# Two decoder layers in one kernel: the up projection's low part of x joins a 512-column product, relative biases are loaded by pairs of heads, and an mLSTM signal is sent earlier

## The reference

```python
# feed-forward of layer one, D_FF = 2816
h = rmsnorm(x, g_ffn) @ w_up                     # (256, 5632)
h = causal_depthwise_conv(h, conv_w, width=3) + conv_b
gate, up = split(h, 2)
y = (gelu(gate) * up) @ w_down

# block attention, S = one block of 256
logits = q @ k.T / 8 + table[:, rel_bucket(q_pos - k_pos)]   # causal
p = softmax(logits)

# mLSTM, per head, after num/den and a norm per head
y_h = (norm(h) * head_norm_g + skip * conv) * silu(z)
```

## Time and profile before

| | us |
|---|---|
| median of 3 runs | 782.49 (782.23 to 783.82) |
| profiled execution, its own time | 784.3 |
| its span, first to last instruction | 782.5 |
| PE busy | 771.3 (99%) |
| DVE busy | 568.2 (73%) |
| ACT busy | 439.1 (56%) |
| POOL busy | 151.0 (19%) |

### The profile page before, as it was taken

The page is one execution under the profiler, slowest core; times in us unless marked ns, Lnnn a source line. Parts: engine busy times, 40 slices in busy tenths (PEclk is TensorE's granted clock), DMA queues, the critical chain, the costliest instruction groups (busy, mean ns, idle before and its releaser), DMA issues.

```text
span 782.5 us, 12013 instructions
## 1 busy us (share of the span) xinstructions
PE 771.3 (99%) x4640; PEld 683.1 (87%) x4640; DVE 568.2 (73%) x916; ACT 439.1 (56%) x609; POOL 151.0 (19%) x112
## 2 busy tenths in 40 slices
PE   9999999999999999999999999999999989999998
PEld 8787778888888899999998889999799878978886
DVE  5755565894558678878784469899875896898785
ACT  6854675345444566566563363566656344889751
POOL 0002930000000004444543000534105000007000
DMA  9986544344455465455455536437475416554311
GB/s 339 406 308 230 168 155 162 112 159 162 161 170 207 163 206 203 175 175 203 164 199 179 212 113 228 144 113 255 157 248 183 162 55 215 199 179 161 108 55 54
DMA packets 23364, 141.77 MB, mean 181 GB/s; under 512 B 3692, under 2 KB 4600, under 8 KB 7440
## 3 DMA queue, kind: packets, MB, share of 16 engines
q1 hardware_dynamic: 20160, 134.51, 48.5%
q0 software_dynamic: 1376, 3.43, 1.3%
q10 hardware_dynamic: 1776, 3.10, 1.1%
HBM read 139.96 MB, written 2.64 MB: 182 GB/s over the span
## 4 chain that ended last, share of the span: by engine, by line
PE 77%; DVE 9%; DMA 7%; ACT 2%; issue 2%; POOL 1%; SPq 0%; ACTq 0%; DVEq 0%
PE gemm L497 14%; PE gemm L499 14%; PE gemm L498 14%; PE gemm L503 9%; PE gemm L505 9%; PE gemm L504 9%; DMA raw<-in_weights 3%; DMA bias_rows<-bias_row 3%; DVE wlo L1733 2%; DVE xc L2320 1%; ACT whi L1198 1%; PE head L561 1%; POOL wsum_p L2515 1%; PE head L794 1%; DMA bias<-bias_rows 1%
## 5 line engine op out<-in xcount | busy, mean ns | idle before, releaser
L1733 DVE TENSOR_TENSOR wlo<-raw,whi 128x2048 fp32r<-128x2048 f32 x119 | 277.5, 2333 | 92.8 <-ACT whi L1198 92.5
L1198 ACT CAST whi<-raw 128x2048 fp32r<-128x2048 f32 x120 | 228.9, 1908 | 196.5 <-PE gemm L499 107.7
L497 PE MATMUL gemm<-whi,x0hi 128*128 128x512 f32 (+2 forms) x368 | 145.0, 394 | 0.7 <-DVE wlo L1733 0.7
L499 PE MATMUL gemm<-whi,x0lo 128*128 128x512 f32 (+2 forms) x368 | 141.5, 385 | 0.0
L498 PE MATMUL gemm<-wlo,x0hi 128*128 128x512 f32 (+2 forms) x368 | 141.2, 384 | 0.0
L503 PE MATMUL gemm<-x1hi,whi 128*128 128x256 f32 x400 | 113.6, 284 | 0.1
L505 PE MATMUL gemm<-x1hi,wlo 128*128 128x256 f32 x400 | 113.2, 283 | 0.0
L504 PE MATMUL gemm<-x1lo,whi 128*128 128x256 f32 x400 | 113.2, 283 | 0.0
L497 PEld LDWEIGHTS gemm<-whi,x0hi 128*128 128x128 f32 x368 | 69.1, 188 | 15.5 <-issue 2.0
L499 PEld LDWEIGHTS gemm<-whi,x0lo 128*128 128x128 f32 x368 | 69.1, 188 | 13.6
L498 PEld LDWEIGHTS gemm<-wlo,x0hi 128*128 128x128 f32 x368 | 69.2, 188 | 12.2
(11 more groups left out here) (377 smaller groups left out, 1342.2 us busy)
## 6 DMA issues: line engine op xcount, KB each, us to landing
raw<-in_weights SPq DMA_DIRECT2D x122, 1024.0 KB, 4.8
raw<-in_weights SPq DMA_DIRECT2D x4, 512.0 KB, 6.3
bias_rows<-bias_row POOLq DMA_DIRECT2D x1, 1536.0 KB, 20.8
memt<-in_memt SPq DMA_DIRECT2D x4, 256.0 KB, 5.3
tok<-in_mem SPq DMA_DIRECT2D x1, 1024.0 KB, 7.2
xt<-in_xt SPq DMA_DIRECT2D x2, 512.0 KB, 11.0
xres<-in_x ACTq DMA_DIRECT2D x1, 1024.0 KB, 9.1
bias<-bias_rows POOLq DMA_DIRECT2D x8, 128.0 KB, 4.4
```

Of the source, the lines that this page charges most:

```text
L497: mm(o, xh, wh, start=start, stop=False)
L499: return mm(o, xl, wh, start=False, stop=stop)
L1198: nc.scalar.copy(whi[:, p % RING, :], raw[:, p % RING, :]).then_inc(s_hi, 1)
L1733: V.tensor_tensor(wlo[:, p % RING, :], raw[:, p % RING, :], whi[:, p % RING, :].bitcast(F32), ALU.subtract).then_inc(s_lo, 1)
```

## The change

- In pieces 2 to 21 of the up projection (`SIDES`), the high and low parts of x lie in one tensor `x1`, and `both_sides` makes one product of whi with both parts (512 columns, one bank per b: the left half gets whi x hi, the right one whi x lo) and one of wlo x hi (256 columns, added to the left half). A chunk takes both banks of its pair.
- ACT copies the two right halves to `u_lo`, ahead of the cast of piece p + 2; DVE adds the left halves and `u_lo` into `u_up`, waits for that, and multiplies by `rrow` in place. ACT's convolution start waits for the latter (`s_scaled`).
- The copy to `scratch` is made by pairs of heads, each followed by a wait and the loads of its two tiles. DVE waits for the tiles of each pair.
- `ml_turn` waits for `s_mread`, which is raised by the second read of the bank.
- `keep_awake` has 12 matmuls; the first product waits only for the first block of the memory's high part; the loops over tokens and blocks within a half piece are swapped.

```diff
-        [[x0hi, x0lo], [_x0, xt], [u_up], [v_ml]] = overlay(
+        [[x0hi, x0lo], [_x0, xt], [u_up, u_lo], [v_ml]] = overlay(
...
+            [("x1", [P, 2, KB, S], F32R)],
...
+        x1hi, x1lo = x1[:, 0, :, :], x1[:, 1, :, :]
...
+        PAIRS = [ctx.enter_context(nc.psum_tensor(f"gemm{i}", [P, 2, 512], F32)) for i in range(2)]
+        G = [PAIRS[i // 2][:, i % 2, :] for i in range(4)]
...
+            def both_sides(o, r, b):
+                for kb in range(KB):
+                    ws = slice(b * P + kb * 2 * P, b * P + kb * 2 * P + P)
+                    mm(o.rearrange("p (a s) -> p a s", a=2), whi[:, r, ws], x1[:, :, kb, :], start=kb == 0, stop=False)
+                    i = mm(o[:, 0:S], wlo[:, r, ws], x1[:, 0, kb, :], start=False, stop=kb == KB - 1)
                 return i
...
             def ml_turn(h):
                 pe.wait_ge(s_mn, h + 1)
                 if h >= 1:
-                    pe.wait_ge(s_mya, h)
+                    pe.wait_ge(s_mread, h)
...
-                for _ in range(16):
+                for _ in range(12):
...
-                        pe.wait_ge(s_inhi, pair + 1)
+                        if (p, half) == (0, 0):
+                            pe.wait_ge(s_in0, 1)
+                        else:
+                            pe.wait_ge(s_inhi, pair + 1)
...
+                elif name == "up" and i_ in SIDES:
+                    c = c0(name) + i_
+                    chunk_free(pe, c - 2)
+                    for b in range(2):
+                        i = both_sides(bank(c, b), r, b)
...
+                        if n in SIDES:
+                            act.wait_ge(s_scaled, SIDES.index(n) + 1)
...
             for p in range(Z0):
+                if p - 1 - p0("up") in SIDES:
+                    act.wait_ge(s_mm, p)
+                    nc.scalar.copy(u_lo[:, :, :], PAIRS[(c0("up") + p - 1 - p0("up")) % 2][:, :, S:2 * S])                        .then_inc(s_side, 1)
...
-                        if h == 0:
-                            dve.wait_ge(s_bias, 16 * MOBA_H)
+                        if h % 2 == 0:
+                            dve.wait_ge(s_bias[h // 2], 32)
...
-                    order(i)
+                    i.then_inc(s_mread, 1)
+                    dve.wait_ge(s_mread, h + 1)
...
+                        if name == "up" and n in SIDES:
+                            dve.wait_ge(s_side, SIDES.index(n) + 1)
+                            V.tensor_tensor(dst, PAIRS[c % 2][:, :, 0:S], u_lo[:, :, :],
+                                            ALU.add).then_inc(s_emptied["dve"], 1)
+                            chunk_free(dve, c)
+                            V.tensor_tensor(dst, dst, rrow[:, :].unsqueeze(1).broadcast_to([P, 2, S]),
+                                            ALU.mult).then_inc(s_scaled, 1)
+                            continue
...
+            for k in range(MOBA_H // 2):
+                pair = slice(2 * k, 2 * k + 2)
+                pool.dma_start(scratch[pair, :].rearrange("h (p n) -> h p n", p=P),
+                               rows_out[pair, :].unsqueeze(1).broadcast_to([2, P, TRI])).then_inc(s_rbd, 16)
+                pool.wait_ge(s_rbd, 32 + 16 * k)
+                for h in (2 * k, 2 * k + 1):
+                    pool.dma_start(bias[:, h, :], scratch[h, P - 1:P - 1 + P * (TRI - 1)]
+                                   .rearrange("(p n) -> p n", p=P)[:, 0:S]).then_inc(s_bias[k], 16)
```

More of the change, by code:

```diff
@@ L30 @@
 POOL_W = 16
+SIDES = list(range(2, 22))
 PAD = POOL_W // 2
@@ L267, in program @@
         ybt = om[:, :, :].rearrange("p t (n s) -> p (t n) s", s=512)
-        G = [ctx.enter_context(nc.psum_tensor(f"gemm{i}", [P, 512], F32)) for i in range(4)]
+        PAIRS = [ctx.enter_context(nc.psum_tensor(f"gemm{i}", [P, 2, 512], F32)) for i in range(2)]
+        G = [PAIRS[i // 2][:, i % 2, :] for i in range(4)]
         A = [ctx.enter_context(nc.psum_tensor(f"head{i}", [P, 512], F32)) for i in range(4)]
@@ L294, in program @@
         s_xt = [s_xt, sem("x_columns_loaded_2")]
+        s_in0 = sem("first_input_hi")
         s_gain, s_onehot = sem("gains_loaded"), sem("onehot_loaded")
@@ L299, in program @@
             "squares_summed", "turned", "turned_hi", "turned_lo"))
-        s_rb, s_rbs, s_rbd, s_bias = (sem(n) for n in (
-            "rel_rows", "rel_rows_copied", "rel_rows_stored", "bias_loaded"))
+        s_rb, s_rbs, s_rbd = (sem(n) for n in ("rel_rows", "rel_rows_copied", "rel_rows_stored"))
+        s_bias = [sem(f"bias_loaded_{k}") for k in range(MOBA_H // 2)]
         s_jt, s_jte, s_js, s_jse, s_jx, s_jp, s_jpe, s_jo, s_jn = (sem(n) for n in (
@@ L331, in program @@
         s_rc = sem("rotary_loaded")
+        s_side, s_scaled = sem("up_side_copied"), sem("up_scaled")
+        s_mread = sem("ml_turned_read")
         s_zero, s_wsum = sem("zeros_ready"), sem("window_sums_ready")
@@ L1024, in first_pieces @@
                         pe.wait_ge(s_hi if half else s_hi0, p + 1)
-                        pe.wait_ge(s_inhi, pair + 1)
+                        if (p, half) == (0, 0):
+                            pe.wait_ge(s_in0, 1)
+                        else:
+                            pe.wait_ge(s_inhi, pair + 1)
                         order_ = [(t, 2 * pair + j, slice((2 * half + j) * 512, (2 * half + j) * 512 + 512))
-                                  for t in range(T) for j in range(2)]
+                                  for j in range(2) for t in range(T)]
                         for t, kb, ws in order_:
+                            if (p, kb, t) == (0, 1, 0):
+                                pe.wait_ge(s_inhi, 1)
                             mm(o[t][:, :], x1hi[:, kb, t * P:t * P + P], whi[:, p % RING, ws], start=kb == 0, stop=False)
@@ L1301, in input_hi @@
                         last = nc.scalar.activation(hi[:, kb, :], src[:, kb, :], ACT.Copy, scale=pcol(col, kb))
+                        if name == "mem" and kb == 0:
+                            last.then_inc(s_in0, 1)
                     last.then_inc(s_inhi, 1)
@@ L2471, in _ @@
             pool.wait_ge(s_rbd, 16)
[L2472 to L2477, removed]
-                               .rearrange("(p n) -> p n", p=P)[:, 0:S]).then_inc(s_bias, 16)
+            for k in range(MOBA_H // 2):
[6 more added lines that the diff above has]
+                                   .rearrange("(p n) -> p n", p=P)[:, 0:S]).then_inc(s_bias[k], 16)
             pool.wait_ge(s_rc, 32)
```

7 lines of the change are left out of this document (4 added, 3 removed).

## The result

The changed kernel takes 795.26 us, median of 6 runs (793.89 to 795.84), the kernel before 782.86 (6 runs, 782.23 to 783.82): a ratio of 1.0156, 95% interval 1.0143 to 1.0169. It is 12.4 us slower. The range ended at 779.2; the sign was wrong.

The account below looks back on a forecast made before the run. The prediction took TensorE, busy 99% of the span, as the bound; gains of 4.2 (up projection), 1.7 (biases), 0.7 (mLSTM) and 0.2 (start), 6.8 us together, came off the 782.49 median: forecast 775.7 us, range 774.6 to 779.2.

Parts of the forecast that it names:

- Biases by pairs: Bias copy and loads by two heads: removes PE's stall before the prob transposes near 75; gain 1.7 us.
- The price: POOL's queue: four round trips of some 10 us instead of one; rotary work may end some 3 us later.
- Rival D: Up projection: DVE's addition is shut out by POOL too, loop 6.43 us, 790.3 us in all; chance 0.05.
- the loop of DVE and POOL: Up projection: mutually excluding multiplication, taps, split and POOL operation, 5.54 us a piece, or 5.74 if handovers save nothing.
- Rival C: Biases: the pairs don't remove PE's stall near 75, 777.4 us in all; chance 0.03.
- rival A: Up projection: DVE and POOL's mutual exclusion is the bound at 5.74 us, gain 2.0, 777.9 in all; chance 0.22.
- The 1.7 us won near 75: PE's prob transposes: idle time from late biases, 1.68 us lost, all won back by loading biases in pairs.
- Up projection: Pieces 2 to 21: one matmul fewer per set, 5.55 instead of 5.76 us a piece; gain taken as 4.2 us.
- The tie of DVE with PE: Up projection: the DVE and POOL loop takes 5.54 us a piece, PE 5.55, so the gain is 4.2 us.
- mLSTM: PE's transposes of a head wait only for DVE's reads of PSUM, not its gate product; gain 0.73 us.
- Start: Shorter keep-awake and first product waiting for one block; piece 4 limits it; gain 0.2 us, bounds 0 and 0.26.

Follow-up runs that it names:

- two copies of half: The changed kernel with two bias copies of four heads each instead of four copies of two heads: 779.90 us, ratio 0.9961.
- spread copies: The changed kernel with each quarter bias copy written with the 128 rows, not the two heads, as slowest dimension: 779.88 us, ratio 0.9954.
- the up projection grouped: The kernel before with only the wide up-projection products, eight 512-column ones in a row, then eight 256-column ones: 779.60 us, ratio 0.9958.

## Why the prediction was wrong

**Biases by pairs: this step failed.** The prediction said of a quarter's copy: "Bounds: by bytes 5.2 us, above 20.8; with a fixed part as in the 4.4 us of a 128 KB load I take 9." It took 15.4 (the page's median), from 13.6 to 17.7: POOL's waits of 12.83 to 16.89 and the 0.8 us by which the one copy's 20.8 exceeds its wait of 20.0. Three things went wrong there.
- The price. It scaled a copy by its bytes. What was measured is another thing: with heads as the slowest dimension POOL waited 11.5 to 17.3 us for 2 heads (the changed kernel and the biases by pairs alone), 14.1 and 17.7 for 4, 17.7 to 20.0 for 8; with 128 rows as the slowest dimension 4.4 to 9.2 us for 2 heads and 12.4 for 8. In the first layout a quarter of the bytes took most of the time of the whole; the later of the four copies were the shorter ones, and why is not shown. The Trainium skill, "DMA: Bandwidth & Descriptors", section "Why a DMA increments its semaphore by 16 and not by 1", states the rule: a DMA is put on the largest number of engines up to 16 that divides the slowest dimension of both sides, and software-issued ones with fewer than 16 take turns from a cursor (it also names an exception on trn2 for some direct copies). By it 2 heads get 2 engines, 4 get 4, 8 get 8 (always 192 KB for each), 128 rows 16; and four copies at once get eight different ones. The times agree with this, and so does the overlap of the four copies. No view here shows the 16 engines one by one, so the count is inferred and not shown. A rival stands beside it (below).
- What stood behind it. The prediction named the rotary work ("may end some 3 us later") and its slack (ended near 105.8, wanted at 119.6), but put only its own estimate of 10 us a round trip through that sum. With the measured round trips the last ended at 110.6; 20.6 us of rotary work more gives 131.3, where it was. The uppermost bound, 20.8 us, was carried only to pair 3 of the biases and given 0.01, and the range left it out. An estimate of the edge is (119.6 - 20.6 - 42.8)/4 = 14 us a round trip, four of them from 42.8 and the rotary work behind; with the 26.2 us that this work took in the kernel before, beside a busy DVE (79.64 to 105.83), it is 12.7. Both are far inside the bounds of 5.2 and 20.8.
- The consequence of an idle PE: 12.1 us of standing brought another 1.9 at the 1.2 GHz level. No rival had that term.

The rival to few engines is a cost of the copy's packets. The rows of the software queue (packets, MB, share of 16 engines) of the kernel before, of the two copies of half, of the changed kernel and of its spread copies are:

```profile
q0 software_dynamic: 1376, 3.43, 1.3%
q0 software_dynamic: 2080, 3.44, 1.5%
q0 software_dynamic: 3488, 3.45, 1.6%
q0 software_dynamic: 1120, 3.43, 1.2%
```

Each further copy by heads brings 704 packets, whether it carries four heads or two, all of them under 512 B by the pages' counts; four spread copies have 80 more than one has (1040 in all, in the kernel before with its copy spread). A time that goes with such packets would also be nearly the same for every copy by heads. No run separates the two. What is shown is that the layout decides, and that in the layout by heads the bytes count for little.

Rival D came out on the right side, but by neither of its mechanisms in full: the loop of DVE and POOL was no bound, and pair 3's biases came in time for all that mattered. It was the copy of nearly constant price, through the rotary work. Rival C, that the stall near 75 stays, did not come: PE has no idle there in the changed kernel's trace. (Half way from the forecast to A is 776.8; the prediction has 776.9.)

**The 1.7 us won near 75 are not in the medians.** The forecast took off 782.49 a stall read from an execution of 784.3. DVE began the first bias at 72.73 there; in the execution of the kernel with the mLSTM signal alone, with the same copy, DVE waited 2.35 us instead of 4.31 and PE not at all. Of the five other kernels with the one copy by heads, only the up projection grouped had a PE idle there (0.99 us) in its trace: that execution took 780.93 us, its four other runs 779.45 to 779.76. Spans of the kernel before lay between 780.3 and 783.1 in its later runs, mostly near 781, and its median stayed when the spread copy took the stall away. With the stall gone from most executions anyway, the pairs could win about 0.1 (780.04 with one copy and waits by pairs, against 780.89 - 0.7 for up projection and mLSTM). That the profiled execution stood 1.8 us above the median was written down in the prediction and not used.

**Up projection: mechanism right, its term too large.** The term "20 x 0.213 = 4.3 us", taken at 4.2, measured 2.1 in the changed kernel and 2.1 alone. PE was the bound throughout, without idle. The pace of a set was 0.353 and not 0.227 + 0.120 = 0.347; over 320 sets that is 2.0 us. The prediction had said that the whole would be wrong "if the pace of alternating widths is not the sum of both", and had no row for it. Grouped, the stage wins 3.5. The tie of DVE with PE held: DVE's split ended at 330.31, ACT's copy was there at about 330.3, the addition began at 330.40, the multiplication was stretched from 0.69 to 0.88 us, and one multiplication followed the other after 5.65 us, as PE's pieces did. With the faster grouped order the additions came every 5.59 us and PE still had no idle, so rival A's 5.74 was no floor. The 2.5 ns of fixed cost that the prediction took from the Trainium skill, "TensorE: Matmul & The Clock Gate", section "Wait — 56ns, not 53.3ns?", would have given 0.8 us by its estimate; both versions won more.

**mLSTM:** 0.73 predicted, 0.72 measured alone. **Start:** 0.2 predicted, 0.0 measured alone, within 0.8 us; the first product did start earlier, at 6.60 instead of 7.33, but piece 4 did not (30.23 instead of 30.04), and that was the bound that the prediction had named.

## What to carry to other kernels

Before a transfer is cut into parts, ask what its time depends on, by the slowest dimension too, and write the copy so that this dimension is long; halving the rows of a copy that is cut by rows may halve nothing. Carry both bounds of an unknown wait to everything queued behind it on its engine, not only to its consumer, and compute the value at which it tells. Take no gain off a median that was read as a stall in a slower than median execution.

## What the runs showed of the hardware that was not expected

- POOL waited 11.5 to 17.3 us for 384 KB from DRAM to DRAM on its queue with 2 heads as the slowest dimension, and 4.4 to 9.2 us for the same bytes with 128 rows as the slowest. 1,536 KB in the two layouts: 17.7 to 20.0 us with the 8 heads, and 12.4 us with the rows.
- Alternating a 512-column product on two blocks with a 256-column one costs 0.353 us a pair; in groups of eight 0.349; the sum of the kinds as other stages show them is 0.347.
- After 12 us without matmuls PE ran about 4 us at a granted clock of 0.50, and this was worth 1.9 us.
